# Attention stages of a two-block transformer kernel: scores in pairs, memory halves ahead of the turns, copies ahead of the exponentials

## The reference

```
s  = q @ k.T * scale + mask          # 128 x 128 for t = 0, 128 x 256 for t = 1
m  = max(s)                          # in block 1's SWA also over a sink value
pr = exp(s - m)
o  = (pr / sum(pr)) @ v
```

```
k, v = split(memn @ wkv)             # 256 x 1024 times 1024 x 2048, for each of 2 layers
```

## Time and profile before

| what | value |
|---|---|
| time, median of 3 runs | 1551.29 us (1550.52 to 1552.45) |
| time of the profiled execution | 1550.02 us |
| its span, first to last instruction | 1548.2 us |
| PE busy | 1484.7 us, 96% of the span |
| DVE busy | 1062.9 us, 69% |
| ACT busy | 777.0 us, 50% |
| POOL busy | 123.1 us, 8% |
| mean granted TensorE clock | 0.997 |
| DMA | 265.03 MB, mean 171 GB/s |

### The profile page before, as it was taken

One profiled execution on the slowest core, in us unless ns is written; L12 is line 12 of the kernel. 1 busy time (PEld: TensorE's weight loads), 2 busy tenths in 40 slices (PEclk: granted clock), 3 DMA queues, 4 the chain that ended last, 5 costly groups with the idle time before them and its releaser, 6 DMA issues.

```text
span 1548.2 us, 21682 instructions
## 1 busy us (share of the span) xinstructions
PE 1484.7 (96%) x8433; PEld 1257.4 (81%) x8433; DVE 1062.9 (69%) x1713; ACT 777.0 (50%) x1162; POOL 123.1 (8%) x98
## 2 busy tenths in 40 slices
PE   8989999999899999999999999999999999999997
PEld 5767888888677888877878988888788789888886
DVE  7777588667866787676355566878863455677777
ACT  4563544444554444433665344666545653456563
POOL 0130000000310000011032000000010320000000
PEclk9999999999999999999999999999999999999999
DMA  7524655656335655644625734556536157345551
GB/s 259 198 99 139 218 190 190 213 167 203 106 120 180 228 190 191 230 155 135 191 63 165 245 131 167 191 190 218 180 116 190 47 167 250 132 168 183 189 189 65
DMA packets 184429, 265.03 MB, mean 171 GB/s; under 512 B 7368, under 2 KB 139398, under 8 KB 184200
## 3 DMA queue, kind: packets, MB, share of 16 engines
q1 hardware_dynamic: 178712, 258.38, 50.2%
q10 hardware_dynamic: 5616, 5.26, 1.0%
HBM read 258.38 MB, written 5.24 MB: 170 GB/s over the span
## 4 chain that ended last, share of the span: by engine, by line
PE 74%; DVE 14%; ACT 4%; issue 3%; DVEq 3%; POOL 1%; ACTq 0%; POOLq 0%; DMA 0%; SPq 0%
PE psw L815 18%; PE psw L814 8%; PE psw L742 7%; PE psw L744 7%; PE psw L743 7%; DVE wlo L1740 5%; PE psa L742 4%; PE psa L744 4%; PE psa L743 4%; PE psa L876 3%; PE psa L874 2%; POOL rstd L2395 1%; DVE sy L1826 1%; PE psa L929 1%; PE psw L818 1%
## 5 line engine op out<-in xcount | busy, mean ns | idle before, releaser
L1740 DVE TENSOR_TENSOR wlo<-raw,whi 128x2048 fp32r<-128x2048 f32 (+3 forms) x199 | 449.6, 2265 | 125.5 <-ACT whi L1352 125.0
L815 PE MATMUL psw<-xboth,whi 128*128 128x512 f32 x1344 | 465.0, 396 | 1.9 <-DVE wlo L1740 1.9
L1352 ACT ACTIVATE whi<-raw 128x2048 fp32r<-128x2048 f32 (+3 forms) x199 | 375.0, 1885 | 178.4 <-PE psw L744 90.5
L814 PE MATMUL psw<-xboth,wlo 128*128 128x256 f32 x1176 | 328.1, 279 | 0.0
L815 PEld LDWEIGHTS psw<-xboth,whi 128*128 128x128 f32 x1344 | 242.8, 188 | 50.3 <-DVE wlo L1740 3.4
L814 PEld LDWEIGHTS psw<-xboth,wlo 128*128 128x128 f32 x1176 | 221.7, 189 | 7.5
L742 PE MATMUL psw<-whi,xboth 128*128 128x512 f32 (+3 forms) x472 | 182.7, 387 | 6.9 <-DVE wlo L1740 5.3
L744 PE MATMUL psw<-whi,xboth 128*128 128x512 f32 (+3 forms) x472 | 179.3, 380 | 0.0
L743 PE MATMUL psw<-wlo,xboth 128*128 128x512 f32 (+3 forms) x472 | 179.3, 380 | 0.0
L1414 ACT ACTIVATE r<-psw 128x512 f32<-128x512 f32 x88 | 52.2, 594 | 173.2 <-PE psw L815 164.2
L742 PE MATMUL psa<-whi,rr 128*128 128x512 f32 x352 | 137.7, 391 | 1.4 <-DVE rr L2370 1.4
(11 more groups left out here) (290 smaller groups left out, 2183.2 us busy)
## 6 DMA issues: line engine op xcount, KB each, us to landing
raw<-in_w_gu SPq DMA_DIRECT2D x44, 1024.0 KB, 5.1
raw<-in_ffn_w_up SPq DMA_DIRECT2D x42, 1024.0 KB, 5.1
raw<-in_w_down SPq DMA_DIRECT2D x22, 1024.0 KB, 4.9
raw<-in_ffn_w_down SPq DMA_DIRECT2D x22, 1024.0 KB, 4.9
raw<-in_w_in SPq DMA_DIRECT2D x20, 1024.0 KB, 5.3
raw<-in_xa_wkv SPq DMA_DIRECT2D x16, 1024.0 KB, 5.4
raw<-in_w_o SPq DMA_DIRECT2D x8, 1024.0 KB, 5.1
raw<-in_w_out SPq DMA_DIRECT2D x8, 1024.0 KB, 5.3
```

The source lines that it names most:

```text
L814: pe.matmul(bank[:, 0:S], wl[:, k, cols], xhi[:, k, :], start=False, stop=False)
L815: ins = pe.matmul(bank.rearrange("p (i s) -> p i s", i=2), wh[:, k, cols], xboth[:, :, k, :], start=k == 0, stop=k == KD - 1)
L1352: nc.scalar.activation(tile_flat("hi", i), tile_flat("raw", i), ACT.Copy).then_inc(hi_ready, 1)
L1740: v.tensor_tensor(tile_flat("lo", i), tile_flat("raw", i), tile_flat("hi", i).bitcast(F32), ALU.subtract).then_inc(lo_ready, 1)
```

## The change

Three orders are changed, and two tables of steps. No product, exponential or copy is added or left out.

1. PE forms the scores of halves i and i+1 together at even steps from step 2 on (halves 0 and 1 still in steps 0 and 1). At odd steps from 3 on there are no scores.
2. PE does the memory half ahead of the turns of its step: at odd steps first of all (in block 2's step 5 behind a wait for the copy of the compressed probabilities, which lie in the same bank), at even steps behind PV.
3. ACT does the filler, the copies of the turned probabilities and the copy of the memory half ahead of the exponentials of its step. The memory half is sent behind the exponentials.
4. The splits of the first weight tiles stand in other steps.

```diff
-HI_STEPS = {1: (7, 8, 9), 2: (10, 11, 13)}
-LO_STEPS = {1: (8, 9, 10), 2: (12, 13, 14)}
+HI_STEPS = {1: (6, 8, 9), 2: (10, 12, 13)}
+LO_STEPS = {1: (7, 9, 10), 2: (11, 13, 14)}
@@ PE, attention: the scores of one half are now a function scores(i) @@
                 for i in range(first, first + count + 3):
-                    if i < first + count:
-                        ... the scores of half i
-                    half_ahead = block == 2 and i - first == SLOTS2[0]
-                    if not half_ahead:
-                        filler(i - first)
+                    if i < first + count and (i % 2 == 0 or i == first + 1):
+                        scores(i)
+                    if i % 2 == 0 and first < i < first + count:
+                        scores(i + 1)
                     half_now = memory_slot(block, l, i - first)
-                    if half_ahead:
+                    if half_now is not None and i % 2:
+                        if block == 2 and i - first == CMP_STEPS[2] + 1:
+                            filler(i - first)
                         half_in_step(half_now)
+                    if block == 1 or i - first != CMP_STEPS[2] + 1:
                         filler(i - first)
                     ... PV of halves i - 4 and i - 3 at even steps
+                    if half_now is not None and i % 2 == 0:
+                        half_in_step(half_now)
                     ... the turns of half i - 2
-                    if not half_ahead and half_now is not None:
-                        half_in_step(half_now)
@@ ACT, memory_store: the sending is now a function memory_send(n, place) @@
+                if send:
+                    memory_send(n, place)
@@ ACT, attention @@
                     ... the high part of the mixed output
+                    filler(i - first)
+                    ... the copies of the turned probabilities of half i - 2
+                    half = memory_slot(block, l, i - first)
+                    if half is not None:
+                        memory_store(half, stage[block - 1][:, half % 2, :], send=False)
                     ... the exponentials of half i
-                    filler(i - first)
-                    ... the copies of the turned probabilities of half i - 2
-                    half = memory_slot(block, l, i - first)
                     if half is not None:
-                        memory_store(half, stage[block - 1][:, half % 2, :])
+                        memory_send(half, stage[block - 1][:, half % 2, :])
                     if i - first in HI_STEPS[block]:
                         serve(memory_key(block, l, HI_STEPS[block].index(i - first)))
```

More of the change, by code:

```diff
@@ L893, in attention, with scores @@
                 count = 2 * sum(1 for x in units if x[0] == block and x[1] == l)
-                for i in range(first, first + count + 3):
-                    if i < first + count:
[L896 to L906, removed]
-                    half_ahead = block == 2 and i - first == SLOTS2[0]
-                    if not half_ahead:
-                        filler(i - first)
+                def scores(i):
+                    u, hf = divmod(i, 2)
+                    kind, t = units[u][2:]
+                    nk = (t + 1) * P
+                    if i >= 2:
+                        pe.wait_ge(smax_done, i - 1)
+                    for b in range(2):
+                        for a in range(2):
+                            h = a * 4 + hf * 2 + b
+                            ins = pe.matmul(psw[:, 2 * (i % 2) + a, b * S:b * S + nk],
+                                            qT(kind, h, t), kT(kind, h, nk), start=True, stop=True)
+                    ins.then_inc(scores_done, 1)
+                for i in range(first, first + count + 3):
+                    if i < first + count and (i % 2 == 0 or i == first + 1):
+                        scores(i)
+                    if i % 2 == 0 and first < i < first + count:
+                        scores(i + 1)
                     half_now = memory_slot(block, l, i - first)
-                    if half_ahead:
+                    if half_now is not None and i % 2:
+                        if block == 2 and i - first == CMP_STEPS[2] + 1:
+                            filler(i - first)
                         half_in_step(half_now)
+                    if block == 1 or i - first != CMP_STEPS[2] + 1:
                         filler(i - first)
@@ L1418, in p_out, with memory_store @@
                 nc.scalar.activation(pT[l], bank2(psw, bank), ACT.Copy).then_inc(p_ready, 1)
-            def memory_store(n, place, src=psa[:, 3, 0:TC]):
+            def memory_store(n, place, src=psa[:, 3, 0:TC], send=True):
                 if n % 2:
@@ L1428, in memory_store, with memory_send @@
                 nc.scalar.activation(place, src, ACT.Copy).then_inc(kv_staged, 1)
+                if send:
+                    memory_send(n, place)
+            def memory_send(n, place):
                 act.wait_ge(kv_staged, n + 1)
@@ L1443, in attention @@
                                                  ACT.Copy).then_inc(mix_hi, 1)
+                    filler(i - first)
+                    if first <= i - 2 < first + count:
+                        n = i - 2
+                        for m in range(chunk0[n], chunk0[n + 1]):
+                            act.wait_ge(pt_done, m + 1)
+                            if m >= 4:
+                                owner = max(x for x in range(len(chunk0) - 1) if chunk0[x] <= m - 4)
+                                act.wait_ge(pv_done, owner + 1)
+                            nc.scalar.activation(pt[:, m % 4, :], psa[:, m % 2, :], ACT.Copy).then_inc(pt_ready, 1)
+                    half = memory_slot(block, l, i - first)
+                    if half is not None:
+                        memory_store(half, stage[block - 1][:, half % 2, :], send=False)
                     if i < first + count:
```

## The result

The changed kernel takes 1538.9 us (median of four runs, 1537.23 to 1541.96) against 1550.91 us in the same comparison: ratio 0.9923, interval 0.9903 to 0.9943. In a later comparison with five rounds the same kernel took 1536.75 us against 1551.23: 0.9903, 0.9889 to 0.9917. The forecast was 1540.4 us, range 1535.5 to 1548.0, a ratio of 0.993.

What follows compares the result with a forecast made beforehand. PE, busy 96% of 1548.2 us, was taken to bound the kernel. 2 x 2.6 + 2 x 3.35 = 11.9 us, less hand-offs 10.9; from 1550.02 that gives 1539.1, plus 1.27 1540.4 us; range 1535.5 to 1548.

Steps and rivals of the forecast that it cites:

- Scores in pairs: Block 1, step 2: scores of two halves together add no work; PE waits 1.0 us for the maxima.
- Memory half ahead of the turns: Block 1: it covers the 1.13 us ahead of turns 3; PE waits 1.0 us in step 3 for its copy.
- Copies ahead of the exponentials: Block 1: exponentials come behind turned blocks; those of half 3 reach DVE with no margin, delaying it 0.15 us.
- Split in step 6: Block 1: ACT's split, 1.91 us, stands ahead of the copy of turned half 5; PE waits 1.8 us.
- The end of the stages: Each block 1 stage's last PV ends 2.6 us earlier, each block 2 stage's 3.35 us earlier.
- my ceiling: All PE idle time in the four stages, 22.3 us; a change of order can give back no more.
- The send: ACT's sends behind the exponentials take 0.46 us as before; nothing waits, and the last comes 2 us earlier.
- Splits and POOL: Block 2's last POOL multiplication, 3.88 us against 1.90, is no longer stretched; in block 1 DVE waits 0.6 us.
- (a): Rival: block 1 gives nothing, only block 2's 2 x 3.35 us is left, 1544.6 us; chance 0.20.
- (b): Rival: all PE waits in the stages go, 22.3 us, giving 1529.0 us; chance 0.04.
- (c): Rival: the 11 us reappear as waits because a load or the send holds the next stage, 1551 us; chance 0.09.
- (d): Rival: exponentials pay for a whole memory half in block 1's steps 3 and 7, 10.0 us slower, 1561.3; chance 0.09.

Runs made afterwards that it cites:

- n_steps: The changed kernel with block 1's old split steps and block 2's new ones: 1533.90 us, ratio 0.9888.
- core: The kernel before with only two edits, the memory half ahead of the turns and ScalarE's new order: 1536.99 us, ratio 0.9908.

## Why the prediction was right

**Scores in pairs, nothing added.** Right for the wait: 1.0 us for the maxima in step 2 measured 0.99, and taking the pairs away changed nothing in the time (0.9901 against 0.9903). What I had missed is that two halves' scores together take less than one and one; see the end of the stages.

**Memory half ahead of the turns.** Right, with the wait for the copy at 0.96 for 1.0. Alone it is worth 7.4 us in the median, 5 or 10 in the single executions.

**Copies ahead of the exponentials, the edit with a cost.** Right in its mechanism: the exponentials of half 3 reach DVE with no margin (its denominators start 0.12 us later behind the maxima than before) and cost nothing more. What the prediction did not say is how much the two edits need each other: -7.4 and +12.1 us alone, -14.2 together.

**Split in step 6.** Right: 1.94 us for 1.8, ahead of the PV of half 5 (I had it ahead of that of half 4), and n_steps gets part of it back. I had not asked whether the old table would be better; it is, in block 1.

**The end of the stages.** Block 1 forecast at 44.4 us, measured 43.83 at full clock; block 2 at 58.8, measured 57.64. So the gain at full clock is 3.3 and 4.54 us where I had 2.6 and 3.35: the sum of the stages is 15.6 us, not 11.9, of which I had even taken off 1.0 for hand-offs.

The mis-sized term is the distance from start to start, which I had taken over from the old order. It was not the waits: block 2 has 2.03 us left where I had 1.65, block 1 3.89 where I had 3.8. Between the kernel before and the changed one, block 2's stage lost 2.96 us of waits and 1.57 us of distances: 1.04 in the scores, by the pairs (1.10 or 1.93 us for two halves, not 2 x 0.64 or 2 x 1.06), 0.28 in the memory halves (3.45 us ahead of turns, as from 814.36 to 817.81, not 3.55) and 0.22 in PV. Against the forecast this makes the 1.19 us: 1.57 less the 0.38 of waits that I had too few. In block 1, layer 1, waits give 2.51 us and distances 0.84. So the premise of my ceiling, that a change of order can give back only what TensorE waits for, was wrong too: over a quarter of the stages' gain at full clock was never idle time.

The send was right: I took it as cost-neutral behind the exponentials, and it is. Sent at once it would have cost 0.54 us in block 2 (58.18 against 57.64, the wait for POOL being 1.07 instead of 0.53) and 0.4 in block 1.

**Splits and POOL.** Right: the 3.88 us became 1.90, the low part of step 7 took 2.53 instead of 2.29 because it had to wait for POOL, and nobody waited for it. With the old steps the 3.88 came back. It also qualifies what I wrote at the start, that semaphores are the only thing that ties one engine's list to another's: here two engines held each other up without one (2.53 us for 2.29, 3.88 for 1.90).

**The clock.** This the prediction did not have. It took full speed for granted, since the earlier trace rows show 1.00 in all four stages. The profiled execution loses 4.8 us to stretches at half clock (45.52 - 43.83, 45.31 - 43.83, 59.28 - 57.64), so 15.6 became 10.8; the kernel before lost 1.36 between its stages, and that was counted as gain. That the total lands 1.5 us from the forecast is therefore luck in good part: a gain that was a quarter too small (11.9 of 15.6) and a cost of 4.8 us that was not foreseen cancel. The mechanism and the waits were right, the size was not. The spread says the same: four executions with a mean clock of 0.994, 0.993, 0.991 and 0.991 took 1537.23, 1537.26, 1540.54 and 1541.96 us.

None of the rivals came. Against (a): block 1 gave 3.3 us at full clock. (b) would need no waits; 11 to 12 us are left. (c): the time between the stages is equal within 0.05 us but for the 1.36 us of clock. (d): DVE never waited more than 0.2 us for denominators in block 1.

What stays open: why some orders have stretches at half clock and others none. Before the falls TensorE had waits of 0.6 to 2 us and short products and turns (70, 107, 435, 762 us); but the kernel before has the same 1.1 us wait at 71 us, and waits of up to 2.43, without a fall, and the changed kernel's place changes from one execution to the next. That filling the waits would remove them wasn't tried. It is open too why the memory half ahead of the turns alone falls into two groups of times.

## What to carry to other kernels

Where an engine's list has work that needs nothing beside work that waits for a chain of others, put the free work first, and then look at who copies its result: here the order on TensorE and the order of the copies on ScalarE took 14 us off together; apart the first took off 7 and the second added 12. Ask of each copy what is queued behind its bank, and of a split or a send what short copy stands behind it. Write the new order out for one stage by start-to-start distances of the trace; it gave each wait within 0.45 us. Then ask what each piece of work has as its new neighbour: the scores of two halves in a row took 0.18 or 0.19 us less than apart, and such distances made 1.6 of the 4.5 us that block 2's stage gained.

## What was not expected of the hardware

TensorE's granted clock fell to half for some 3.4 us at a time, in places that changed between executions of one kernel. It cost 1.5 to 1.7 us in most places in the stages, 1.36 at 700 us in the kernel before, and 0.1 at the start of block 1's stages, where TensorE had a wait to give up. The longest wait ahead of such a fall in the changed kernel was 1.94 us, in others 3.4. A kernel whose trace has none in its stages (core, 0.9908, 1536.72 to 1537.35 us) and one with three or four (the changed kernel, 0.9903, 1533.89 to 1537.32) come out level, though the second's stages are shorter by 0.4 us in block 1 and 0.7 in block 2 at full clock.
